# Memory attention of prompt and sample in one interleaved block instead of two blocks in a row

## The reference, cut to what matters

```python
def cross_attn(h, mk, mv, w_qg, w_o):
    q, g = jnp.split(h @ w_qg, 2, axis=-1)
    s = jnp.einsum('bthd,bmhd->bhtm', q, mk) * (X_HEAD_DIM ** -0.5)
    p = jax.nn.softmax(s, axis=-1)
    o = jnp.einsum('bhtm,bmhd->bthd', p, mv).reshape(b, t, D_MODEL)
    return (o * jax.nn.silu(g)) @ w_o
```

## Time and profile before

| | us |
|---|---|
| median of 3 runs | 3266.49 (3266.34 to 3270.77) |
| profiled execution | 3262.93 |
| its span, first to last instruction | 3261.3 |
| first score matmul to last write of SGX, layer 0 | 1323.71 to 1457.24 |
| the same, layer 1 | 3010.75 to 3146.46 |

### The profile page before, as it was taken

One profiled execution on the slowest core, in us unless ns is written; L12 is line 12 of the kernel. 1 busy time (PEld: TensorE's weight loads), 2 busy tenths in 40 slices (PEclk: granted clock), 3 DMA queues, 4 the chain that ended last, 5 costly groups with the idle time before them and its releaser, 6 DMA issues. The chain is left out here.

```text
span 3261.3 us, 42138 instructions
## 1 busy us (share of the span) xinstructions
PE 2800.3 (86%) x16534; PEld 2214.1 (68%) x16534; DVE 1566.6 (48%) x2711; ACT 820.4 (25%) x1492; POOL 589.3 (18%) x436
## 2 busy tenths in 40 slices
PE   5997858869988899889799959977599999699789
PEld 4996645547667699658699947754455554599567
DVE  3999625645544400353466551026677774300353
ACT  3223324442222312322222221111212221321221
POOL 2221220012312222013221201000222121221012
PEclk8998879989997899989899979988699989799999
DMA  2311550025530021150222222137442330121151
GB/s 87 98 46 35 171 188 1 1 76 191 176 131 1 13 72 46 58 206 1 44 99 81 76 82 75 69 81 243 129 116 77 96 72 1 39 72 60 53 191 47
DMA packets 237204, 277.40 MB, mean 85 GB/s; under 512 B 44870, under 2 KB 183815, under 8 KB 231316
## 3 DMA queue, kind: packets, MB, share of 16 engines
q1 hardware_dynamic: 217234, 186.84, 18.9%
q0 software_dynamic: 16384, 75.77, 6.5%
q10 hardware_dynamic: 3456, 12.98, 1.0%
HBM read 230.51 MB, written 45.47 MB: 85 GB/s over the span
## 5 line engine op out<-in xcount | busy, mean ns | idle before, releaser
L305 PE MATMUL pp<-HH,WS_part 128*128 128x352 f32 x1824 | 589.8, 323 | 0.0
L303 PE MATMUL pp<-HH,WH 128*128 128x352 f32 x1344 | 436.9, 325 | 30.1 <-POOL WS_part L444 30.1
L304 PE MATMUL pp<-HT_part,WH 128*128 128x352 f32 x1344 | 434.9, 324 | 0.0
L305 PEld LDWEIGHTS pp<-HH,WS_part 128*128 128x128 f32 x1824 | 345.9, 190 | 0.0
L303 PEld LDWEIGHTS pp<-HH,WH 128*128 128x128 f32 x1344 | 254.7, 190 | 31.9 <-POOL WS_part L444 31.9
L2658 PE MATMUL OP<-oWO,YT 128*128 128x512 f32 (+1 forms) x576 | 255.7, 603 | 3.3 <-DVE XE L2785 3.3
L304 PEld LDWEIGHTS pp<-HT_part,WH 128*128 128x128 f32 x1344 | 254.8, 190 | 0.0
L444 POOL TENSOR_TENSOR WS_part<-WS,WH 128x1024 fp32r<-128x1024 f32 x56 | 143.1, 2555 | 504.3 <-ACT WH L395 504.3
L816 DVE SCALAR_TENSOR_TENSOR CV<-GX,cw,CV x360 | 215.9, 677 | 0.0
L2658 PEld LDWEIGHTS OP<-oWO,YT 128*128 128x128 f32 (+1 forms) x576 | 105.0, 184 | 146.1 <-issue 142.6
L1976 DVE TENSOR_REDUCE xmx<-xS 128x4 f32<-128x1024 f32 x16 | 19.5, 1219 | 376.1 <-PE xS L1937 376.1
(11 more groups left out here) (490 smaller groups left out, 5354.3 us busy)
## 6 DMA issues: line engine op xcount, KB each, us to landing
WS<-x_w_qg SPq DMA_DIRECT2D x32, 512.0 KB, 4.0
HT<-cache_mem_k SPq DMA_DIRECT2D x16, 1024.0 KB, 8.3
HT<-cache_mem_v POOLq DMA_DIRECT2D x16, 1024.0 KB, 8.0
CBt<-cum_scratch SPq DMA_DIRECT2D x8, 2048.0 KB, 10.1
xbc_scratch<-oACC ACTq DMA_DIRECT2D x24, 528.0 KB, 2.7
WS<-o_w_in SPq DMA_DIRECT2D x24, 512.0 KB, 3.9
XT<-xbc_scratch SPq DMA_DIRECT2D x8, 1536.0 KB, 7.6
WS<-e_w_in SPq DMA_DIRECT2D x20, 512.0 KB, 3.9
```

What stands on the lines that cost most here:

```text
L303: nc.tensor.matmul(out, wh, xh, start=start, stop=False)
L304: nc.tensor.matmul(out, wh, xl, start=False, stop=False)
L305: return nc.tensor.matmul(out, wl, xh, start=False, stop=stop)
```

## The change

`cross_prompt` and `cross_sample` become one block, `cross_both`. Sequence i is worked on together with prompt tile i, in an order that is written out for each engine. The sample's loads go to the space of `HT` from the start of the block; `PT` gets space of its own (one tile). The value slot `VB` is single, where there were two; the key slots stay two; the transposed keys have one place, `KBT`. Of the prompt's PSUM, `S` is single (two banks), the transposed probabilities go through one bank `TB` in two halves, which the sample's transposes use as well, and the value products go through one bank `PO`, four groups of 128 columns at a time; the keys' transposes alternate between two banks. The prompt's values are multiplied per tile (128 columns per matmul) and no longer per four tiles (512). The sample's score matmuls run over heads inside and halves outside. The four scalings per tile become one multiply with a broadcast. The rest is as it was.

The new order per engine and the new waits, cut from the diff:

```diff
+            S, TB, PO = pb(c, "xS", (P, XH * MEM)), pb(c, "xT"), pb(c, "xO")
+            ZT, ZS, ZO = [pb(c, f"zT{a}") for a in range(2)], pb(c, "zS"), pb(c, "zO")
+            @block.sync
+                for b in range(NB):
+                    if b >= 2:
+                        sp.wait_ge(z_tp, 4 * (n0 + b - 1))
+                    sp.dma_start(KB[b % 2], ck[:, b]).then_inc(z_l[b % 2], 16)
+            @block.gpsimd
+                for b in range(NB):
+                    if b:
+                        pool.wait_ge(z_pv, n0 + b)
+                    pool.dma_start(VB, cv[:, b]).then_inc(z_lv, 16)
             @block.tensor
                 def scores(i):
-                    if i >= 2:
-                        pe.wait_ge(x_ex, XH * (n0 + i - 1))
+                    if i:
+                        pe.wait_ge(x_ex, XH * (n0 + i))
...
+                def turn(i, r):
+                    if r:
+                        pe.wait_ge(x_te, 2 * (n0 + i) + 1)
+                    else:
+                        pe.wait_ge(x_pn, n0 + i + 1)
+                        if i >= 2:
+                            pe.wait_ge(z_pe, n0 + i - 1)
...
+                def values(i, r):
+                    pe.wait_ge(x_te, 2 * (n0 + i) + 2)
+                    pe.wait_ge(x_oe, 2 * (n0 + i) + r)
+                    for d in range(4 * r, 4 * r + 4):
                         for k in range(2):
+                            m = nc.tensor.matmul(PO[:, (d % 4) * P:(d % 4 + 1) * P], VM[:, k, d * P:(d + 1) * P], PT[:, (d // 2) * 2 + k, :],
...
+                def keys(b, q):
+                    if q == 0:
+                        pe.wait_ge(z_l[b % 2], 64 * l + 16 * (b // 2 + 1))
+                    if q >= 2:
+                        pe.wait_ge(z_te, 4 * (n0 + b) + q - 1)
+                    elif b:
+                        pe.wait_ge(z_te, 4 * (n0 + b - 1) + q + 3)
+                def sample_scores(b):
+                    pe.wait_ge(z_te, 4 * (n0 + b) + 4)
...
+                def sample_values(b):
+                    pe.wait_ge(z_pe, n0 + b + 1)
+                    pe.wait_ge(z_lv, 16 * (n0 + b + 1))
...
                 scores(0)
                 for i in range(NQ):
                     if i + 1 < NQ:
                         scores(i + 1)
+                    keys(i, 0)
+                    keys(i, 1)
+                    turn(i, 0)
+                    keys(i, 2)
+                    turn(i, 1)
+                    keys(i, 3)
+                    sample_scores(i)
+                    values(i, 0)
+                    if i:
+                        sample_turn(i - 1)
+                    values(i, 1)
+                    if i:
+                        sample_values(i - 1)
+                sample_turn(NB - 1, True)
+                sample_values(NB - 1)
...
             @block.vector
+                    nc.vector.tensor_tensor(PB[v][:], PB[v][:], ri[:, v, :].unsqueeze(2).to_broadcast([P, XH, MEM]), ALU.mult).then_inc(x_pn, 1)
...
+                normalise(0)
                 for i in range(NQ):
+                    keys_out(i, 0)
+                    keys_out(i, 1)
+                    keys_out(i, 2)
                     if i + 1 < NQ:
                         maximum(i + 1)
+                    keys_out(i, 3)
+                    sample_maximum(i)
+                    outputs(i, 0)
+                    if i + 1 < NQ:
+                        normalise(i + 1)
+                    sample_normalise(i)
+                    outputs(i, 1)
...
             @block.scalar
                 for i in range(NQ):
+                    turned(i, 0)
+                    turned(i, 1)
                     if i + 1 < NQ:
                         exponent(i + 1)
+                    sample_exponent(i)
+                    if i:
+                        sample_turned(i - 1)
```

More of the change, by code:

```diff
@@ L1938, in scores @@
                                                  KM[:, 2 * h + k, :], start=k == 0, stop=k == 1)
                     m.then_inc(x_sc, 1)
[L1941 to L1945, removed]
+                def turn(i, r):
[5 more added lines that the diff above has]
+                            pe.wait_ge(z_pe, n0 + i - 1)
+                        elif i:
+                            pe.wait_ge(x_te, 2 * n0 + 2)
+                    for h in range(2 * r, 2 * r + 2):
@@ L1946, in turn @@
                         for k in range(2):
-                            t = nc.tensor.transpose(TPp[:, (2 * h + k) * P:(2 * h + k + 1) * P],
-                                                    PB[i % 2][:, h, k * P:(k + 1) * P], ident[:])
+                            n = 2 * (h % 2) + k
+                            t = nc.tensor.transpose(TB[:, n * P:(n + 1) * P], PB[i % 2][:, h, k * P:(k + 1) * P], ident[:])
                     t.then_inc(x_tp, 1)
[L1951 to L1956, removed]
+                def values(i, r):
+                    pe.wait_ge(x_te, 2 * (n0 + i) + 2)
+                    pe.wait_ge(x_oe, 2 * (n0 + i) + r)
+                    for d in range(4 * r, 4 * r + 4):
@@ L1957, in values @@
                         for k in range(2):
[L1958 removed]
+                            m = nc.tensor.matmul(PO[:, (d % 4) * P:(d % 4 + 1) * P], VM[:, k, d * P:(d + 1) * P], PT[:, (d // 2) * 2 + k, :],
                                                  start=k == 0, stop=k == 1)
[L1960 removed]
+                    m.then_inc(x_pv, 1)
+                def keys(b, q):
[5 more added lines that the diff above has]
+                        pe.wait_ge(z_te, 4 * (n0 + b - 1) + q + 3)
+                    for k in range(2):
+                        for n in range(2):
+                            t = nc.tensor.transpose(ZT[q % 2][:, (2 * k + n) * P:(2 * k + n + 1) * P],
+                                                    KB[b % 2][:, n, (2 * q + k) * P:(2 * q + k + 1) * P], ident[:])
+                    t.then_inc(z_tp, 1)
@@ new lines, in sample_scores @@
+                def sample_scores(b):
+                    pe.wait_ge(z_te, 4 * (n0 + b) + 4)
+                    if b:
+                        pe.wait_ge(z_ex, n0 + b)
+                    for k in range(2):
+                        for h in range(XH):
+                            m = nc.tensor.matmul(ZS[32 * h:32 * h + 32, 0:MEM], QT[:, 2 * h + k, TP:TOK], KBT[:, 2 * h + k, :],
+                                                 start=k == 0, stop=k == 1, tile_position=(0, 32 * h), skip_group_check=True)
+                    m.then_inc(z_sc, 1)
@@ new lines, in sample_turn @@
+                def sample_turn(b, last=False):
+                    pe.wait_ge(z_pn, n0 + b + 1)
+                    if last:
+                        pe.wait_ge(z_pe, n0 + b)
+                    else:
+                        pe.wait_ge(x_te, 2 * (n0 + b + 1) + 2)
+                    for k in range(2):
+                        t = nc.tensor.transpose(TB[:, k * P:(k + 1) * P], PZ[b % 2][:, k * P:(k + 1) * P], ident[:])
+                    t.then_inc(z_pt, 1)
+                def sample_values(b):
+                    pe.wait_ge(z_pe, n0 + b + 1)
+                    pe.wait_ge(z_lv, 16 * (n0 + b + 1))
+                    for k in range(2):
+                        for h in range(XH):
+                            m = nc.tensor.matmul(ZO[32 * h:32 * h + 32, 0:XD], PZT[:, k, 32 * h:32 * h + 32],
+                                                 VB[:, k, h * XD:(h + 1) * XD], start=b == 0 and k == 0,
+                                                 stop=b == NB - 1 and k == 1, tile_position=(0, 32 * h), skip_group_check=True)
+                    m.then_inc(z_pv, 1)
@@ L1965, in _ @@
                         scores(i + 1)
[L1966 to L1969, removed]
+                    keys(i, 0)
[13 more added lines that the diff above has]
+                sample_values(NB - 1)
+                pe.wait_ge(z_oe, 3 * l + 1)
+                for k in range(2):
+                    t = nc.tensor.transpose(TB[:, k * P:(k + 1) * P], OS[:, k * P:(k + 1) * P], ident[:])
+                t.then_inc(z_pt, 1)
             @block.vector
@@ new lines, in _ @@
+                dve.wait_ge(z_pv, n0 + NB)
+                nc.vector.tensor_copy(OS[:], ZO[:, 0:XD]).then_inc(z_oe, 1)
+                dve.wait_ge(z_pt, t0 + NB + 1)
+                heads = SGX[:].rearrange("p (h k) t -> p k h t", k=2)
+                for k in range(2):
+                    part = heads[:, k, :, TP:TOK]
+                    nc.vector.tensor_tensor(part, part, TB[:, k * P:(k + 1) * P].rearrange("p (h t) -> p h t", h=XH),
+                                            ALU.mult).then_inc(z_oe, 1)
```

232 lines of the change are left out of this document (60 added, 172 removed).

## The result

The changed kernel takes 3282.43 us (median of 9 runs, 3277.85 to 3290.15) where the kernel before takes 3268.28 us. The ratio is 1.0045 with a 95% interval of 1.0029 to 1.006: 14 us slower, where 9 were forecast. A second series gave 1.0047 (1.0028 to 1.0065). One of the nine runs of the kernel before took 11914 us, and the ratio leaves it out.

The account below looks back on a forecast made before the run. PE, busy 86% of the span, was taken as the bound. Per layer, block 128.8, key wait 7.5, clock 2.3 and 0.5 make 139.1 us; both layers 278.2 against 269.2, +9.0, giving 3275.5 us, range 3250 to 3296.

Parts of the forecast that it names:

- PE at the first keys 10.56 us after the first score, keys at 18.1, a wait of 7.5: Block start: first keys queue behind WO and gb, so PE waits 7.5 us a layer, bounds 5 and 9.
- An interior iteration of 14.76 us: Merged loop: one interior iteration along its critical chain takes 14.76 us, against 14.40 for its parts before.
- Waits of 1.64 for the last key copy and 0.74 for the bank: Each interior iteration: PE waits 1.64 us for DVE's last key copy and 0.74 for the single value bank.
- A wait of 5.6 us in the tail, 8.6 from the issue on: Block end: the single value slot delays sequence 7's load; PE stands 5.6 us, 8.6 from issue to end.
- 2.3 us of lower clock behind the keys: After the first key wait: PE starts at the lower clock, costing 2.3 us a layer, bounds 1.3 and 4.
- 128-column records at 0.115, bounds 0.107 and 0.16: Prompt's value matmuls: 0.115 us a record, 3.68 a tile; the bounds mean -2 or +11 us a layer.
- Only this part changes.: Whole kernel: only the pair of attention blocks changes, 269.2 us over both layers before.
- (C): Attention blocks: a wash, with pace 0.107, a 5 us key wait and 1.3 of clock; 3264.5 us; chance 0.13.
- (D): Prompt's value matmuls: records run at 0.16 us, 11.5 us more a layer; 3298.5 us; chance 0.11.
- (E): Merged loop: waits drop PE to 1.2 GHz for part of each iteration, 2 us each; 3307 us; chance 0.07.
- (A): Merged loop: PE's waits fill better; all 2.8 us an iteration gone gives 3234 us, half 3254; chance 0.15.
- (B): Block start: first keys don't wait and PE keeps the upper clock, 2 x 9.8 us less; 3256 us; chance 0.07.

Follow-up runs that it names:

- Keys first: Changed kernel with the WO and gb loads issued behind the first two key loads; 3270.73 us, 1.0006 of the kernel before.
- Copy first: Changed kernel with DVE copying the last quarter of the keys before the next tile's maximum; 3276.64 us, 1.0017 of the kernel before.
- PE order: Changed kernel with sample transposes before sample scores, sample values between the prompt's value halves, and ACT's copy earlier; 3273.28 us, 1.0015 of the kernel before.
- All four: Changed kernel with keys before WO and gb, last values in the free key slot, and DVE's, PE's and ACT's orders changed; 3231.94 us, ratio 0.9883.
- both loads edited: Changed kernel with keys ahead of WO and gb and last values in the free key slot, loop orders untouched; 3260.77 us, ratio 0.9977.

## Why the prediction was right

The measured time and its sign came out as forecast, inside the range of 3250 to 3296, and the size was +14 where +9 were named. The mechanism was right too, waits at the edges and in the loop. The blocks of both layers took 285.0 us where 278.2 were named, 6.8 more. Step by step, for layer 0:

- *PE at the first keys 10.56 us after the first score, keys at 18.1, a wait of 7.5.* Keys at 19.3 (1324.71 to 1343.99), a wait of 6.70 in layer 0 and 7.88 in layer 1. PE came later in layer 0 (12.58), since the second scores ran mostly at the lower clock (5.41 us), a cost that had no term of its own and that the wait for the keys hid. The order in the queue and the values between it are as the argument from the earlier trace rows had them: WO landed at 16.8 us and not 14.1, 2.7 later, about what one megabyte takes. The Trainium skill's rule (DMA: Bandwidth & Descriptors, Queues, rings and completion order) agrees with this: WO, gb and the keys, all in SP's ring, landed in their order (16.8, 17.7 and, in the median of two, 20.3 us after their issue), and POOL's values, issued 1.9 us after WO, went beside it and landed first (10.2). "Keys first" showed the cost in the blocks in full: 16.7 us with its clock.
- *An interior iteration of 14.76 us.* 15.19. Scores to sample scores 8.31 against 8.27; the rest spread over runs that I had paced without their starts: sample scores 1.00 for 0.92, two runs of values 1.89 and 1.95 for 1.84, the gap between them 1.04 for 0.99, sample values 1.00 for 0.90. This is the mis-sized term: 0.43 us an iteration. The seven iterations from the second on took 98.56 us where 95.81 were named, in both layers, so that 5.5 of the lacking 6.8 us lie here. The rest is the keys' landing, 1.2 us late in layer 0 and 0.7 in layer 1, and the tail, less what iteration 0 took below its term.
- *Waits of 1.64 for the last key copy and 0.74 for the bank.* 1.50 and 0.65, at the places named. "Copy first" cut the first to 0.78 and "PE order" took the second away; their prices in the blocks were 9.1 and 19.5 us. The latter holds more than the bank, since PE's transposes and their wait moved with it.
- *A wait of 5.6 us in the tail, 8.6 from the issue on.* 5.43 and 5.22; the tail took 9.55 (1457.87 to 1467.42) with its slow records, where 9.1 were named.
- *2.3 us of lower clock behind the keys.* Iteration 0 took 15.32 us (1343.99 to 1359.31) where 13.86 + 2.3 = 16.2 were named, so this term was some 0.8 us too large. From 1359.3 to 1457.8, the rest of the loop, the granted clock was 1.00, as the prediction had it.
- *128-column records at 0.115, bounds 0.107 and 0.16.* 0.113 in an unbroken run, 0.118 and 0.122 in the merged loop with the start of each run. The upper bound, read from the distance to the next instruction, was no price of the record.
- *"Only this part changes."* This step failed in the profiled execution, which took 27.2 us more where 9.0 were named: 9.2 of them sit in the state stage, at a lower clock, and the cause stays open. I had asked for no row of that stage. By the medians (14.2 us) nothing outside the blocks is needed, but the executions behind them have no profile. That the two sums agree so closely may be luck.

Of the rivals, (C) falls with the wait for the keys, 6.70 and 7.88 us where it asked for 5, (D) with the records at 0.12 us, (E) with the clock at 1.00 in the loop. (A) and (B), the faster ones, were not what this kernel does, but the experiments went their way. "Keys first" took 16.7 us off the blocks where (B) named 19.6. "All four" came to 3232, and that (A) had named 3234 is luck: (A) had it all from the loop, 2.8 us an iteration, and the loop gave 1.8 (15.19 to 13.37), about half of the gain; the rest came from the edges. I had taken PE's fixed order as an argument that the waits stay, but that order can be changed, and "PE order" did it.

## What to carry to other kernels

When two stages are merged, follow the first transfer of the new block back through its queue: what was issued ahead of it, and had no reader in a hurry before, now stands in front of one that has. A slot cut from two to one may be free in the loop and still cost one whole load at the last turn. And before a merged loop is given up, list the waits of its slowest engine at its edges and in one iteration. Most can be tried by moving a few lines, and here four such edits turned 0.45% slower into 1.2% faster. Last, look at the stages that the change doesn't touch as well: the profiled executions differed there by as much as 17 us, more than the change itself.

## What was not expected of the hardware

The granted clock of PE in a stage that no edit touched was not the same in every profiled execution. The state stage ran in five patterns, of about 90.4, 91.8, 99.7, 104.6 and 107.2 us, with the same matmuls. The shown periods of 11.5, 13.2, 15.7 and 16.9 us had mean clocks of 1.00, 0.87, 0.72 and 0.60. Of the six profiled executions with the old block in layer 0, five showed the first pattern, and the one with its loops written out did not. Whether program text ahead of the stage sets the pattern, or each execution may fall into any of them, is not settled: it would take several profiles of one kernel, some of them of its longer runs.

The clock behind a wait was not fixed by the wait's length either. Behind the same 3.48 us at the start of the block the sixteen second scores took 5.41 us in layer 0 and 3.72 in layer 1 of the changed kernel, and 6.78 and 6.45 with both loads edited.
